# Quarter-width casting DMAs, a LayerNorm 2 that stores from its residual buffer, four held-back down blocks and a last down projection in two halves

## The reference, cut to what matters

```
p = x @ w_in                      # 1024 -> 7 x 1024: B_a C_a v_a val gate g_a g_b
y_a = (B_a * conv3(C_a * v_a)) @ w_out_a
y_b = silu(LN_c(conv31(val * sigmoid(gate)))) @ w_out_b
x1  = LN_1(alpha * x  + (sigmoid(g_a) * y_a + sigmoid(g_b) * y_b) @ w_o)
x2  = LN_2(alpha * x1 + relu(x1 @ w_up)^2 @ w_down)      # 1024 -> 4096 -> 1024
```

## Time and profile before

| what | value |
|---|---|
| median of three runs | 2259.0 us |
| profiled execution | 2274.43 us |
| its span, core 5 (slowest) | 2272.9 us |
| spans of all cores | 2234.3 to 2272.9 us |
| PE busy | 2177.8 us (96%) |
| DVE, ACT, POOL busy | 868.8, 902.2, 634.5 us |
| queue q0 (POOL's casts) | 14640 packets, 88.15 MB, 23.7% of 16 engines |
| queue q1 (SP) | 82656 packets, 291.53 MB, 42.2% |

### The profile page before, as it was taken

The page is one execution under the profiler, slowest core; times in us unless marked ns, Lnnn a source line. Parts: engine busy times, 40 slices in busy tenths (PEclk is TensorE's granted clock), DMA queues, the critical chain, the costliest instruction groups (busy, mean ns, idle before and its releaser), DMA issues.

```text
span 2272.9 us, 33255 instructions; the slowest of 8 cores (2234.3 to 2272.9 us)
## 1 busy us (share of the span) xinstructions
PE 2177.8 (96%) x11568; PEld 965.6 (42%) x11568; DVE 868.8 (38%) x1199; ACT 902.2 (40%) x1422; POOL 634.5 (28%) x538
## 2 busy tenths in 40 slices
PE   6999999999979889899999999999999999999896
PEld 3444444444434334344444444444444444444342
DVE  2121362722346023651356134803381237322604
ACT  1111231364325523354335533563346334642552
POOL 1000040514234042522343143404350426030321
PEclk9999888999989999999999999999999999999998
DMA  9997659799867997775876557655666556445352
GB/s 154 137 150 140 155 150 163 227 171 165 226 183 171 202 223 201 204 199 136 249 222 179 164 168 218 179 167 176 193 192 169 179 171 206 140 148 185 130 185 74
DMA packets 107827, 400.68 MB, mean 176 GB/s; under 512 B 13712, under 2 KB 54928, under 8 KB 68752
## 3 DMA queue, kind: packets, MB, share of 16 engines
q1 hardware_dynamic: 82656, 291.53, 42.2%
q0 software_dynamic: 14640, 88.15, 23.7%
q10 hardware_dynamic: 10368, 18.88, 2.5%
HBM read 432.07 MB, written 58.79 MB: 216 GB/s over the span
## 4 chain that ended last, share of the span: by engine, by line
PE 82%; DMA 9%; DVE 4%; issue 1%; POOL 1%; ACT 1%; SPq 0%; ACTq 0%; DVEq 0%; POOLq 0%
PE ps L274 78%; PE ps L426 5%; DMA wbf<-wsl 3%; DMA wsl<-wblk 2%; DMA yblk<-tt 2%; DVE sgt L297 1%; DMA h<-wblk 1%; POOL sumQ L284 1%; DMA u0d<-cvb 1%; POOL tt L284 1%; DVE cvb L284 0%; DVE tt L284 0%; DVE sumS L284 0%; DMA wsl<-wbf 0%; DVE u L284 0%
## 5 line engine op out<-in xcount | busy, mean ns | idle before, releaser
L274 PE MATMUL ps<-xbf,wsl 128*128 128x512 bf16 x2624 | 615.3, 388 | 7.0 <-DMA wsl<-wbf 3.6
L274 PE MATMUL ps<-bx,wsl 128*128 128x512 bf16 x2560 | 574.3, 382 | 19.1 <-DMA wsl<-wblk 11.9
L274 PE MATMUL ps<-h,wsl 128*128 128x512 bf16 x2496 | 544.9, 380 | 7.1 <-DMA wsl<-wblk 7.1
L280 ACT ACTIVATE tA<-ps 128x512 f32<-128x512 f32 x448 | 265.0, 594 | 462.4 <-PE ps L274 437.6
L274 PEld LDWEIGHTS ps<-xbf,wsl 128*128 128x128 bf16 x2624 | 256.3, 99 | 334.8 <-issue 71.6
L274 PEld LDWEIGHTS ps<-bx,wsl 128*128 128x128 bf16 x2560 | 249.9, 98 | 330.6 <-issue 42.0
L274 PEld LDWEIGHTS ps<-h,wsl 128*128 128x128 bf16 x2496 | 244.6, 98 | 303.5 <-issue 10.4
L284 POOL TENSOR_TENSOR tt<-tt,rstd 128x512 f32<-128x512 f32 x178 | 244.8, 1376 | 97.5 <-ACT rstd L280 74.7
L284 POOL TENSOR_TENSOR tt<-res,mu 128x512 f32<-128x512 f32 x112 | 157.6, 1407 | 384.3 <-DMA yblk<-tt 225.4
L284 POOL TENSOR_TENSOR tt<-u,mu 128x512 f32<-128x512 f32 x66 | 90.9, 1377 | 567.9 <-ACT mu L280 515.2
L274 PE MATMUL ps<-xbf,h 128*128 128x512 bf16 x1024 | 232.3, 389 | 17.2 <-DMA h<-wblk 16.9
(11 more groups left out here) (68 smaller groups left out, 1159.7 us busy)
## 6 DMA issues: line engine op xcount, KB each, us to landing
wsl<-wbf SPq DMA_DIRECT2D x218, 1024.0 KB, 6.2
wsl<-wblk POOLq DMA_DIRECT2D x38, 1024.0 KB, 14.8
rep<-u0d SPq DMA_DIRECT2D x256, 135.0 KB, 4.2
wbf<-wblk POOLq DMA_DIRECT2D x16, 1024.0 KB, 23.0
wbf<-wsl SPq DMA_DIRECT2D x16, 1024.0 KB, 16.6
yblk<-tt ACTq DMA_DIRECT2D x56, 256.0 KB, 6.1
xbf<-xblk POOLq DMA_DIRECT2D x13, 1024.0 KB, 15.3
xft<-xblk POOLq DMA_DIRECT2D x32, 256.0 KB, 6.7
```

The lines of the kernel that those rows point to most:

```text
L274: last = e.matmul(bank_ap, lhsT=l, rhs=r, start=(start and idx == 0), stop=(stop and idx == n - 1))
L280: S.op("act", lambda e: e.activation(out=out, in_=in_, func=func, bias=bias, scale=scale), reads=reads, writes=writes)
```

## The change

The casting DMAs are issued in four quarters along the row, each on the same semaphore; a waiter waits for all four. Three kinds are changed: `convert`, the cast branch of `w_load`, and `x_load`. LN 2 writes its scaled result back to the residual buffer and stores from there, on one semaphore per chunk. LATE becomes 4, so DN4 to DN7 of pass 6 run in pass 7, and in pass 6 three instead of two chunks of LN c are taken per down block. The last down projection runs all eight blocks on tokens 0 to 255 and again on tokens 256 to 511 (the list of weight blocks gets eight more entries); LN 2 of the first half is applied by POOL and ACT beside the second half's matmuls, that of the second half by DVE and ACT at the end. `ln2_last` is gone.

```
-        LATE = 3
+        LATE = 4
...
+        seq += [DN0 + k for k in range(8)]
...
-                S.dma("pool", castsem[blk], wbf[blk], wblk[blk], writes=[("wbf", blk)])
+                S.dma_batch("pool", castsem[blk], quarters(wbf[blk], wblk[blk]), writes=[("wbf", blk)])
+
+        def quarters(out, in_):
+            return [(out[:, 1024 * k:1024 * k + 1024], in_[:, 1024 * k:1024 * k + 1024]) for k in range(4)]
...
-                S.dma("pool", wcsem[s], wsl[s][:], wblk[blk], writes=[("wsl", s)])
+                S.dma_batch("pool", wcsem[s], quarters(wsl[s][:], wblk[blk]), writes=[("wsl", s)])
...
-            S.dma("pool", xbsem[i % 2], xbf[i % 2][:], xblk[i], writes=[("xbf", i % 2)])
+            S.dma_batch("pool", xbsem[i % 2],
+                        [(xbf[i % 2][:, 2 * k:2 * k + 2, :], xblk[i, :, 2 * k:2 * k + 2, :]) for k in range(4)],
+                        writes=[("xbf", i % 2)])
...
-                act(tt[r][:], tt[r][:], AF.Identity, reads=[("tt", r), "cst"], writes=[("tt", r)],
+                act(buf[:, e_, :], tt[r][:], AF.Identity, reads=[("tt", r), "cst"], writes=[(bid, e_)],
                     bias=pv[:, 6, e_:e_ + 1], scale=pv[:, 5, e_:e_ + 1])
-                S.dma("act", osem[r], yblk[i, :, e_, :], tt[r][:],
-                      reads=[("tt", r)], writes=[("y", i, e_)])
+                S.dma("act", osem[e_], yblk[i, :, e_, :], buf[:, e_, :],
+                      reads=[(bid, e_)], writes=[("y", i, e_)])
...
+        def down_halves(i, R):
+            def chunk(e_, hf):
+                s = w_next(DN0 + e_)
+                mm(ps[b][:, 0:H], [(wsl[s][:, kc * 128:(kc + 1) * 128], h[:, kc, c]) for kc in range(32)],
...
+            for e_ in range(8):
+                chunk(e_, 0)
+            for e_ in range(8):
+                chunk(e_, 1)
+                if e_ == 0:
+                    finish(0)
+                else:
+                    for k_ in ([0, 1] if e_ == 1 else [e_]):
+                        sub(k_, 0, "pool")
+                        scale(k_, 0, "pool")
+                        out(k_, 0)
+            finish(1)
+            for e_ in range(3):
+                sub(e_, 1, "dve")
+            for e_ in range(8):
+                scale(e_, 1, "dve")
+                if e_ + 3 < 8:
+                    sub(e_ + 3, 1, "dve")
+                out(e_, 1)
...
-                down_part(range(8), R, stD)
-                stD.finish(1)
-                ln2_last(i, R)
+                down_halves(i, R)
...
-                        take(lnc_tasks, 2)
+                        take(lnc_tasks, 3 if i == NPASS - 2 else 2)
...
-        S.final_wait("act", [(k, S.dma_cnt[k]) for k in osem])
+        S.final_wait("act", [(k, S.dma_cnt[k]) for k in osem + lsem])
```

More of the change, by code:

```diff
@@ L185, in build_nc @@
         xfsem = [S.new_sem(f"xf{i}") for i in range(8)]
-        osem = [S.new_sem(f"o{i}") for i in range(NTT)]
+        osem = [S.new_sem(f"o{i}") for i in range(8)]
+        lsem = [S.new_sem(f"l{i}") for i in range(8)]
         csem = [S.new_sem(f"k{i}") for i in range(5)]
@@ L485, in fin @@
             def fin():
-                act(tt[r][:], tt[r][:], AF.Identity, reads=[("tt", r), "cst"], writes=[("tt", r)],
+                act(buf[:, e_, :], tt[r][:], AF.Identity, reads=[("tt", r), "cst"], writes=[(bid, e_)],
                     bias=pv[:, 6, e_:e_ + 1], scale=pv[:, 5, e_:e_ + 1])
-                S.dma("act", osem[r], yblk[i, :, e_, :], tt[r][:],
-                      reads=[("tt", r)], writes=[("y", i, e_)])
-            return fin
[L492 to L511, removed]
+                S.dma("act", osem[e_], yblk[i, :, e_, :], buf[:, e_, :],
+                      reads=[(bid, e_)], writes=[("y", i, e_)])
+            return fin
         ln_fin = []
@@ L680, in down_part, with finish, sub, scale @@
                     each(e_)
+        def down_halves(i, R):
+            rbuf, rid = R
+            H = T // 2
+            col = (slice(0, H), slice(H, T))
+            m_, r_, k = mu[1], rstd[1], 1
+            def chunk(e_, hf):
+                c = col[hf]
+                uid = ("uh", e_, hf)
+                s = w_next(DN0 + e_)
+                b = nb()
+                mm(ps[b][:, 0:H], [(wsl[s][:, kc * 128:(kc + 1) * 128], h[:, kc, c]) for kc in range(32)],
+                   reads=[("wsl", s)] + [("h", kc) for kc in range(32)], writes=[("ps", b)])
+                stt(rbuf[:, e_, c], rbuf[:, e_, c], ALPHA, ps[b][:, 0:H], ALU.mult, ALU.add,
+                    reads=[(rid, e_), uid, ("ps", b)], writes=[uid])
+                rel(b)
+                q = rt("sq", 2)
+                act(sq[q][:, 0:H], rbuf[:, e_, c], AF.Square, reads=[uid], writes=[("sq", q)])
+                if e_ == 0:
+                    chunk.first = q
+                elif e_ == 1:
+                    add(sumS[k][:, c], rbuf[:, 0, c], rbuf[:, 1, c], reads=[("uh", 0, hf), uid],
+                        writes=[("sumS", k)])
+                    add(sumQ[k][:, c], sq[chunk.first][:, 0:H], sq[q][:, 0:H],
+                        reads=[("sq", chunk.first), ("sq", q)], writes=[("sumQ", k)])
+                elif e_ < 7:
+                    add(sumS[k][:, c], sumS[k][:, c], rbuf[:, e_, c], reads=[("sumS", k), uid],
+                        writes=[("sumS", k)])
+                    add(sumQ[k][:, c], sumQ[k][:, c], sq[q][:, 0:H], reads=[("sumQ", k), ("sq", q)],
+                        writes=[("sumQ", k)])
+                else:
+                    add(sbf[0][:, c], sumS[k][:, c], rbuf[:, e_, c], reads=[("sumS", k), uid],
+                        writes=[("sbf", 0)])
+                    add(sbf[1][:, c], sumQ[k][:, c], sq[q][:, 0:H], reads=[("sumQ", k), ("sq", q)],
+                        writes=[("sbf", 1)])
+            def finish(hf):
+                c = col[hf]
+                bm, be = nb(), nb()
+                for r, b in ((0, bm), (1, be)):
+                    mm(ps[b][:, 0:H], [(ones[:, :], sbf[r][:, c])], reads=[("sbf", r), "ones"],
+                       writes=[("ps", b)])
+                mid, rid_ = ("mu", 1, hf), ("rstd", 1, hf)
+                act(m_[:, c], ps[bm][:, 0:H], AF.Copy, reads=[("ps", bm), ("mu", 1)], writes=[mid])
+                act(r_[:, c], ps[bm][:, 0:H], AF.Square, reads=[("ps", bm), ("rstd", 1)], writes=[rid_])
+                stt(r_[:, c], ps[be][:, 0:H], EPS, r_[:, c], ALU.add, ALU.subtract,
+                    reads=[("ps", be), rid_], writes=[rid_])
+                act(r_[:, c], r_[:, c], AF.Ln, reads=[rid_], writes=[rid_])
+                act(r_[:, c], r_[:, c], AF.Exp, reads=[rid_], writes=[rid_], scale=-0.5)
+                rel(bm, be)
+            def sub(e_, hf, eng):
+                c = col[hf]
+                tten(eng, rbuf[:, e_, c], rbuf[:, e_, c], m_[:, c], ALU.subtract,
+                     reads=[("uh", e_, hf), ("mu", 1, hf)], writes=[("uh", e_, hf)])
+            def scale(e_, hf, eng):
+                c = col[hf]
+                uid = ("uh", e_, hf)
+                tten(eng, rbuf[:, e_, c], rbuf[:, e_, c], r_[:, c], ALU.mult,
+                     reads=[uid, ("rstd", 1, hf)], writes=[uid])
+            def out(e_, hf):
+                c = col[hf]
+                uid = ("uh", e_, hf)
+                act(rbuf[:, e_, c], rbuf[:, e_, c], AF.Identity, reads=[uid, "cst"], writes=[uid],
+                    bias=pv[:, 6, e_:e_ + 1], scale=pv[:, 5, e_:e_ + 1])
+                S.dma("sp", lsem[e_], yblk[i, :, e_, c], rbuf[:, e_, c],
+                      reads=[uid], writes=[("y", i, e_, hf)])
+            for e_ in range(8):
+                chunk(e_, 0)
+            for e_ in range(8):
+                chunk(e_, 1)
+                if e_ == 0:
+                    finish(0)
+                else:
+                    for k_ in ([0, 1] if e_ == 1 else [e_]):
[10 more added lines that the diff above has]
+                out(e_, 1)
```

## The result

The changed kernel takes 2268.6 us (median of 11 runs, 2260.0 to 2428.25), the kernel before 2259.06 us beside it (11 runs). The ratio is 1.0041 [1.0024, 1.0059]: 9 us slower, where 2212 us, 47 under the median, were forecast. In the ten runs of after that are left, five have two to four cores with a mean granted clock of 0.975 to 0.980 and took 2267.9 to 2278.0 us; the other five took 2260.0 to 2268.6, with a median of 2263. The profiled execution of after is one of the first five; its span is 2265.7 us on core 2.

A forecast was written before the change was run, and what follows sets the result against it. PE, busy 96% of the span, was taken as the bound: matmuls, stalls and lowered clock after them. Terms summed to -44.9 us on core 5; 2262 - 44.9 - 5.4 gave 2212 us, range 2192 to 2234.

The forecast's parts named there:

- Quarter-width casts: Casting DMAs: finer packets end the starvation of stores; 5 us gained in pass 1's up and down, 2 lost in pass 0.
- My price of 10% per byte: Casting DMAs: a quarter row costs 10% more per byte than a whole one, bounds 0% and 32%.
- The small stalls: Waits before the first convolution (4.16 us) and on core 3 for a bf16 block (5.38 us) go: 4 and 5.4 us gained.
- The base of 2262 us: Whole kernel: time without core 5's lowered clock, core 3's 2260.7 us plus 1.5 us around the span.
- The rival of pure capacity: Casts in pass 1: finer packets cost as much as starvation did, up to 14 us lost; 2222 us, chance 22%.
- LN 2 from the residual buffer: Passes 1 and 2: POOL no longer waits for y stores; 16.6 us of stalls and 10.1 of clock, 26.7 us gained.
- Four blocks held back: Before the last up: the 5.79 us stall and 3.8 us of clock go, net gain 6 us; 1 us lost in pass 6.
- The last down in halves: Last down and end: 7.4 us gained after the last matmul, less 0.6 for more waits: 6.8 us (4 to 9).
- fixed price per quarter: Casts of passes 0 and 1: quarters pay a fixed price in a row on POOL's queue; 2317 us, chance 4%.
- y store in stage mix: Stage mix, passes 1 and 2: the y store becomes the wait, 6 us of stall and clock after it; 2226 us, chance 9%.
- The lowered stretch: Whole kernel: one die runs with a lowered clock in the typical run; 2229 us, chance 9%.

The follow-up runs named there:

- after: The changed kernel with all parts of the change, against the kernel before: 2268.6 us, ratio 1.0041.
- late_only: The kernel before with only LATE = 4 and three chunks of LayerNorm c per down block in pass 6: ratio 1.0001.
- late_later: The kernel before with LN 2 from the residual buffer, halved last down, LATE = 4, and LN 2's held-back sums and chunks later in the last up: ratio 0.9883.
- part_split: The changed kernel with each cast in four DMAs of 32 partitions with whole rows instead of quarter rows: ratio 0.9953.
- store_early: The kernel before with LN 2 from the residual buffer, halved last down, and UP7, DN0, DN1 stored as bfloat16 in pass 0 instead of pass 1: ratio 0.988.
- quarters_early: The changed kernel, quarters included, with UP7, DN0 and DN1 stored as bfloat16 in pass 0 instead of pass 1: ratio 0.9982.

## Why the prediction was wrong

**Quarter-width casts: the step that failed.** It read "mostly capacity, some 14 of 26 us; 12 come from starved stores that free slots late", and took a gain of 5 in pass 1. Its observations hold: 182:188 packets became 582:589, the stores wbf<-wsl land in 11.7 us. What did not follow is that PE gains by it. In a stretch where the engines are held 97% of the time, a store that goes first makes a cast go later, and the cast is what PE needs next: 52.7 us of stores and 28.2 of casts in the chain became 58.0 us of casts. No gain shows, and the price stands whole: 5.2 us in up and down 1. The forecast also had the shortage too small. It put casts at 80 us and the rest at 30, in 106 us that PE would need; with whole casts the engines are held 0.98 x 126 = 123 us, 92 of them by casts, and PE needs 116.8 us without a stall (pass 2).

My price of 10% per byte was near the 6 to 8% measured, although its working is off: the terms give 401 ns for a half row, not 399, and the straight line through both points about 25% for a quarter row, not 32%. Where I charged it was wrong. I charged 8 us in pass 1 and 2 in pass 0. The traces show 5.0 us in stage F (token tiles, 2.92 us wait at 163.53), 4.7 in pass 0, 5.2 in pass 1, 2.7 in pass 2, 17.6 in all, less 4.0 in S3 1 to S1A 2; the ratio says 33 us in all, the runs with all clocks over 0.98 say 25. The rest of 7 to 11 us is not explained: the stages are of one execution each, and a stage's median isn't the slowest core's. The small stalls, -4 and -5.4, both shrank where they were read (the first convolution's from 4.16 to 0.7 us on core 5, where whole casts have none either; the one of 5.38 us on core 3 is gone), but new ones came, 2.92 us for a token tile and 4.29 us for a bfloat16 block on core 3 at 412 us, and no gain is left. Forecast for all of it: 12 us gained. Measured: 33 lost. That is 45 of the 57 us of the miss; LN 2 adds 16 and the held-back blocks 5, the last down gives 5 back. The base of 2262 us was 3 us over the median. The rival of pure capacity had the right mechanism, but charged only pass 1, and so gave 2222 us; its own "up to 14 us lost instead of 5 gained" would reach 2231.

**LN 2 from the residual buffer: right in mechanism, too large by 16 us.** The y store is gone from POOL's waits, PE's waits for sums fell from 20.6 us on the slowest core to 5.3, and no wait on a y store appears in stage mix. But 26.7 us were read on core 5, which had the largest stall (11.3 us where cores 0, 2, 3 and 7 had 7.3 to 8.2 at the longest), mixed with a lowered clock, and then taken off a base that stood for core 3. Alone it is 0.9951, 11 us: the medians give 4.9 in S3 1 to S1A 2 and 5.0 a pass later, and 7.42 us came back on one core as a wait for a bfloat16 block. I had looked for what is late next only in stage mix, not in SP's queue within S3.

**Four blocks held back: forecast -5, measured 0.** The stall of 5.79 us went. I had put what queues on DVE behind LN 1 at 3 us, and after shows 2.91. What was mis-sized is the rest: I counted 3.8 us of clock as given back, but up 7 grew by about the new stall and more (57.5 to 61.0 us in late_only), and the stages from up of pass 6 to mix of pass 7 fell by 3.9 us for 6.9 us of matmuls less, a loss of 3.0, with one 3.03 us wait for ACT at the start of pass 7, where I had 1 us. In late_later, which delays those sums and the chunks of LN 2, the stages get the 5 us back (up 7 at 57.4 with the halves, 62.7 in after).

**The last down in halves: right, on the low side.** From the last matmul to the end 22.1 became 11.8 us, 10.3 gained where the steps gave 7.4. 512 matmuls of 256 columns take 56.3 us, 110 ns each, 0.9 us more than 256 of 512 (forecast 0.6). PE waits for no block in the last down on any core. Alone it is 0.9951, 11 us.

**The rivals.** No fixed price per quarter (part_split). No y store in stage mix. The lowered stretch, given 9%, is in the profile and in five of ten runs of after, which are about 9 us longer than the others. What the forecast lacked was a rival in which the quarters are charged wherever PE runs on casts just landed, stage F and pass 2 included.

## What to carry to other kernels

Before reordering transfers against each other, ask how full the DMA engines are in that stretch: at 0.97 here only engine time per byte and bytes counted, so keep rows long and move bytes to stretches with room. The test is the chain of waits before and after the reordering: if the same time only changes its owner, order was not the limit. A transfer taken out helps only if it stood ahead of the stall. Price a change of transfers in every stage that consumes them just in time, not only where the worst stall is. Read a stall on all cores, not on the slowest alone, and don't add two gains that cure the same wait.

## What the runs showed of the hardware

- A casting DMA from float32 costs engine time by the width of its rows: 6.2 us of all 16 engines per MB written at 8 KB, 6.3 at 4 KB, 6.65 at 2 KB, 7.4 at 1 KB, in up and down of pass 1, beside a second queue. The price is that of a crowded stretch: with three casts less, the same rows cost 5.9 at 8 KB (store_early) and 6.3 at 2 KB (quarters_early).
- The total time grew less for eighths (51 us over whole rows) than the price per MB suggests by the quarters (33 us for 7%, 20% for the eighths). Packets overlap in the records (share 1.07), so part of the held time may not be lost; that was not tested, and each total is good to about 12 us.
- Two queues with work alternate by packets, not by bytes or time: 182:188 with casts of 0.92 us, 582:589 with quarters.
- Four queued casts of a quarter of the partitions each cost little more than one of the whole: 6.1 and 6.2 us per MB, 13 us (-1 to 27) in the whole kernel for 201 DMAs more.
- 256 matmuls of 512 columns take 55.4 us, 216 ns each, and 512 of 256 columns 56.3 us, 110 ns each, with a full weight load before every one.
